# One level of Strassen's algorithm in the last stage of a hybrid encoder block, with activations passed through DRAM

## The chip, the cores and the metric

The kernel runs on one core of a Trainium2 chip. The time is the device time of one launch in microseconds (us). PE is TensorE (matmuls), DVE is VectorE, ACT is ScalarE, POOL is GpSimd, SP is SyncE, which here only issues DMAs. SBUF is the on-chip memory of 128 partitions, PSUM the accumulators that matmuls write, DRAM the memory outside the core.

## The reference, cut to what matters

Sequence 2048, width 1024, feed-forward width 4096, all float32.

```python
mix = jnp.concatenate([att.reshape(bsz, s, ATTN_WIDTH), ssm], axis=-1)   # each 512 wide
h = h + mix @ w_out[l]                                # 1024 x 1024
hn2 = rmsnorm(h, norm2_g[l])
h = h + jnp.square(jax.nn.relu(hn2 @ w_mlp1[l])) @ w_mlp2[l]   # 1024 x 4096, 4096 x 1024
return rmsnorm(h, final_g)
```

`att` is the attention output after an RMS norm over each head's 128 values; `ssm` is `z * sigmoid(z @ w_glu + b_glu)`, the gate. Both are made in earlier stages.

## The kernel before

Four stages follow each other, each a block with its own queues for the five engines: the projection, attention, the state space model with its gate (`phase_ssm`), and the last stage (`phase_mlp`), which computes the lines above. Only the last part of `phase_ssm` and the whole of `phase_mlp` are changed.

Values are kept transposed: features on the 128 partitions, tokens along the columns. Every float32 product of the last stage is made of three matmuls in the faster format fp32r: a value is split into a high part (ACT copies it with rounding) and a low part (DVE subtracts the high part from the value), and high x high, high x low and low x high are added in PSUM.

`phase_mlp` goes through four blocks of 512 tokens (`tb`). In each, `out` makes eight 128-row tiles of `mix @ w_out` and adds `x`; then come two halves of the feed-forward layer: 16 pieces `up` (1024 to 128 features, then relu squared) and two times eight pieces `down`, which collect in four PSUM banks. All activations of a block stay in SBUF. The weights are read once per block of tokens, in pieces of 128x1024 (512 KB) through four buffers `w_raw`; ACT and DVE split each piece (`split_high`, `split_low`) while TensorE uses the one before it. POOL squares and adds `h` for the norm, 128x512 at a time, and issues the loads of `mix` and `x` and the stores of `y`. The norm's factor is applied after `up` and `down`, since relu squared scales with its square, and so stands in nobody's way.

The attention outputs reach the stage with tokens on the partitions. DVE scales them (`mix_scale`), TensorE turns them in four 128x128 transposes a head (`turn_mix`), ACT copies them back with the gain (`mix_back`); for the blocks after the first this lies beside the `up` and `down` pieces.

The gate, the end of `phase_ssm`, has 16 rounds (4 blocks of tokens x 4 tiles of features): TensorE makes `z @ w_glu` into `y_ps`, ACT the sigmoid into `gate`, DVE the product with `z` into `out`, SP stores `out` to `ssm_s`. `y_ps`, `gate` and `out` have two buffers each.

Engines take their instructions in the order in which they are written, and wait for semaphores in that order too.

Of the kernel before, what the change touches and what calls it, by code (L numbers as in the profile page):

```python
# [7 lines left out]

# [8 lines left out]
F32 = mybir.dt.float32  # L17
# [7 lines left out]
P = 128  # L25
# [1122 lines left out]
def phase_ssm(nc, head, mag, s_d, cp_s, w_glu, b_glu, z_s, ssm_s):  # L1148
# [13 lines left out]
    NPAIR = NGR * 2  # L1162
    with ExitStack() as ctx:
# [21 lines left out]
        out = m.sb("out", [P, 2, TB])  # L1185
        w_ps = m.ps("w_ps", [P, 2, 2, NJ])
# [27 lines left out]
        out_stored = [m.sem("out_stored0"), m.sem("out_stored1")]  # L1214
        block = ctx.enter_context(nc.Block())
# [32 lines left out]
        def _(sp):  # L1248
# [21 lines left out]

            sp.dma_start(d_in[:], s_d).then_inc(d_loaded, 16)
# [4 lines left out]
            for n in range(NGR):  # L1276
# [11 lines left out]
                if n == 3:  # L1288
                    sp.dma_start(wg[:], w_glu).then_inc(glu_loaded, 16)
                    sp.dma_start(bg[:], b_glu).then_inc(glu_loaded, 16)  # L1290
                if n + XR < NGR:
# [8 lines left out]
            for n in range(4 * NTB):  # L1300
                tb, c = n // 4, n % 4
                sp.wait_ge(out_ready, n + 1)
                sp.dma_start(ssm_s[c, :, tb * TB:(tb + 1) * TB], out[:, n % 2]).then_inc(out_stored[n % 2], 16)
            for i in range(2):
                sp.wait_ge(out_stored[i], 16 * 2 * NTB)

# [35 lines left out]
        def _(act):  # L1342
# [29 lines left out]

            for t in range(4):
                turned_b(0, t)
# [13 lines left out]
            for n in range(4 * NTB):  # L1388
# [4 lines left out]
                    .then_inc(gate_ready, 1)  # L1393

        @block.vector
        def _(dve):
# [25 lines left out]

            for step in range(NPAIR + 3):
# [9 lines left out]
            for n in range(4 * NTB):  # L1433
# [4 lines left out]
                if n >= 2:  # L1438
# [4 lines left out]
                    .then_inc(out_ready, 1)  # L1443

        @block.tensor
        def _(pe):
# [69 lines left out]
            for n in range(NGR - 3, NGR):  # L1516
                outputs(n)
            pe.wait_ge(glu_loaded, 32)
            for n in range(4 * NTB):
# [9 lines left out]
                last.then_inc(glu_done, 1)  # L1529


def phase_mlp(nc, x_t, att_s, att_square, att_floor, ssm_s, w_stream, gains, y_t):
# [13 lines left out]
    PIECE = 1024  # L1546
    RAW = 4
    TURNS = 18
    OUT_TURNS, UP_TURNS, DOWN_TURNS = 2, 4, 2
    HALF_TURNS = UP_TURNS + 2 * DOWN_TURNS  # L1550
    OUTS, DOWNS = OUT_TURNS * RAW, DOWN_TURNS * RAW
    MIX_ORDER = list(range(H, KD)) + list(range(H))
    Y_TILES = {5: (0, 1, 2), 6: (3, 4, 5), 7: (6, 7)}
    NC = TB // P
    LAM_INIT = 0.8 - 0.6 * math.exp(0.0)
    with ExitStack() as ctx:
        m = Memory(nc, ctx, "ml")
        w_raw = m.sb("w_raw", [P, RAW, PIECE])
        w_hi = m.sb("w_hi", [P, 2, PIECE], F32R)
        w_lo = m.sb("w_lo", [P, 2, PIECE], F32R)  # L1560
        act_hi = m.sb("act_hi", [P, 16, TB], F32R)
        act_lo = m.sb("act_lo", [P, 16, TB], F32R)
        hg_hi = m.sb("hg_hi", [P, KD, TB], F32R)
        hg_lo = m.sb("hg_lo", [P, KD, TB], F32R)
        h = m.sb("h", [P, KD, TB])
        x_in = m.sb("x_in", [P, KD // 2, TB])
        h_out = m.sb("h_out", [P, KD, TB])
        mix = m.sb("mix", [P, KD, TB])
        relu = m.sb("relu", [P, 2, TB])
        relu_sq = m.sb("relu_sq", [P, 2, TB])  # L1570
        product_in = relu_sq
        square = m.sb("square", [P, TB])
        sums = m.sb("sums", [P, TB])
        square2 = m.sb("square2", [P, TB])
        sums2 = m.sb("sums2", [P, 2, TB])
        inv_var = m.sb("inv_var", [P, TB])
        total = m.sb("total", [P, H, S // P])
        rinv_att = m.sb("rinv_att", [P, H, NC])
        inv_c = m.sb("inv_c", [P, NC])
        rms_c = m.sb("rms_c", [P, NC])  # L1580
        gain = m.sb("gain", [P, 2 * KD + 1])
        gain_att = m.sb("gain_att", [P, 1])
        ones = m.sb("ones", [P, 1])
        ident = m.sb("ident", [P, P])
        eps_c = m.sb("eps_c", [P, 1])
        work = m.ps("work", [P, 2, TB])
        down = m.ps("down", [P, 4, TB])
        spread = m.ps("spread", [P, 2, TB])
# [48 lines left out]
        def static(x):  # L1637
            return isinstance(x, int)
# [621 lines left out]
```

## Time and profile before

| | us |
|---|---|
| time, median of 3 runs | 2972.96 |
| lowest and highest of them | 2971.13, 4062.39 |
| span of the profiled execution (first to last instruction) | 2969.5 |
| last stage, from SP's first DMA issue to the end of the span | 1315.2 to 2969.5 |
| its matmuls, first start to last start | 1331.5 to 2940.3 |
| busy in the span: PE / DVE / ACT / POOL | 2781.0 / 1696.7 / 1196.7 / 358.4 |

The profiled execution's own time isn't listed beside the three; its span is 1.6 us under the lowest of them and 3.5 us under the median. Busy time of PE is not time at full speed: matmuls overlap in the pipeline, so what one costs is read from the distance between starts.

### The profile page before, as it was taken

What the parts mean: (1) busy time and instruction counts of PE and PEld (TensorE: products, weight loads), DVE (VectorE), ACT (ScalarE), POOL (GpSimd) and SP (SyncE); (2) the same over time, 40 slices, a digit from 0 to 9 for tenths busy, and PEclk for the clock granted to TensorE, in tenths of its full rate; (3) what the DMA queues carried; (4) which work ended last, traced back from release to release, by engine and by line L of the source; (5) the groups of instructions that cost most, each with busy time, mean ns of one, the idle gap of its engine ahead of it and who ended that gap; (6) DMA issues with size and microseconds to landing.
All of it is one profiled execution on the core that took longest, in us unless ns stands there. A gap on an engine that the chain in (4) does not pass through costs nothing.

```text
span 2969.5 us, 37537 instructions
## 1 busy us (share of the span) xinstructions
PE 2781.0 (94%) x13704; PEld 2319.9 (78%) x13704; DVE 1696.7 (57%) x2363; ACT 1196.7 (40%) x1847; POOL 358.4 (12%) x300
## 2 busy tenths in 40 slices
PE   6978796999999979979999999999999999999996
PEld 5757585999999967737888878888888888788885
DVE  7665517999999947635434365443554343743434
ACT  3365515878787731123323223233233232232331
POOL 5230001101010013303000121000130001300001
PEclk9989898999999989989999999999999999999998
DMA  5335524020220049634232334232252222332322
GB/s 168 139 144 204 183 72 112 22 66 23 65 72 22 17 133 283 165 142 142 92 99 93 98 99 170 92 99 92 93 177 96 95 98 93 101 124 95 99 93 70
DMA packets 160980, 322.41 MB, mean 109 GB/s; under 512 B 30160, under 2 KB 87760, under 8 KB 157136
## 3 DMA queue, kind: packets, MB, share of 16 engines
q1 hardware_dynamic: 143568, 265.58, 29.0%
q10 hardware_dynamic: 10368, 29.89, 2.7%
q0 software_dynamic: 6912, 25.17, 2.3%
q8 instruction: 84, 1.38, 0.2%
q14 instruction: 48, 0.39, 0.0%
HBM read 255.05 MB, written 63.44 MB: 107 GB/s over the span
## 4 chain that ended last, share of the span: by engine, by line
PE 49%; DVE 3%; DMA 1%; issue 1%; POOL 0%; ACT 0%; DVEq 0%; POOLq 0%; ACTq 0%
PE ml_work L2087 9%; PE ml_work L2089 8%; PE ml_work L2088 8%; PE ml_down L2089 8%; PE ml_down L2087 8%; PE ml_down L2088 8%; DMA ml_x_in<-in_x_t 1%; DVE ml_w_lo L1762 1%; PE ml_spread L2050 0%; DVE ml_h L1899 0%; DVE ml_h_out L1888 0%; DMA ml_mix<-att_s 0%; DVE ml_hg_lo L1903 0%; DVE ml_h_out L1974 0%; ACT ml_w_hi L1758 0%
## 5 line engine op out<-in xcount | busy, mean ns | idle before, releaser
L1762 DVE TENSOR_TENSOR ml_w_lo<-ml_w_raw,ml_w_hi 128x1024 fp32r<-128x1024 f32 x288 | 369.1, 1281 | 797.4 <-ACT ml_w_hi L1758 797.3
L1758 ACT ACTIVATE ml_w_hi<-ml_w_raw 128x1024 fp32r<-128x1024 f32 x288 | 305.2, 1060 | 1033.7 <-PE ml_down L2089 542.2
L2087 PE MATMUL ml_work<-ml_hg_hi,ml_w_hi 128*128 128x512 f32 x1024 | 399.5, 390 | 0.8 <-DVE ml_w_lo L1762 0.8
L2087 PE MATMUL ml_down<-ml_act_hi,ml_w_hi 128*128 128x512 f32 x1024 | 399.0, 390 | 0.0
L2089 PE MATMUL ml_work<-ml_hg_hi,ml_w_lo 128*128 128x512 f32 x1024 | 398.5, 389 | 0.0
L2088 PE MATMUL ml_work<-ml_hg_lo,ml_w_hi 128*128 128x512 f32 x1024 | 398.4, 389 | 0.0
L2089 PE MATMUL ml_down<-ml_act_hi,ml_w_lo 128*128 128x512 f32 x1024 | 398.4, 389 | 0.0
L2088 PE MATMUL ml_down<-ml_act_lo,ml_w_hi 128*128 128x512 f32 x1024 | 398.4, 389 | 0.0
L886 ACT ACTIVATE at_e<-at_e,at_neg_top 128x2048 f32<-128x2048 f32 x128 | 256.6, 2005 | 37.0 <-DVE at_neg_top L971 37.0
L1081 PEld LDWEIGHTS at_pv<-at_v,at_a_t 128*128 128x128 f32 x2048 | 257.5, 191 | 16.4
L1081 PE MATMUL at_pv<-at_v,at_a_t 128*128 128x128 f32 x2048 | 258.9, 275 | 0.0
L1054 PE MATMUL at_score<-at_k_hi,at_q_hl 128*128 128x512 f32 x512 | 225.1, 440 | 20.7 <-DVE at_q_hl L948 17.7
L2087 PEld LDWEIGHTS ml_work<-ml_hg_hi,ml_w_hi 128*128 128x128 f32 x1024 | 192.3, 188 | 41.6 <-issue 1.4
L2089 PEld LDWEIGHTS ml_work<-ml_hg_hi,ml_w_lo 128*128 128x128 f32 x1024 | 192.2, 188 | 40.2
L2089 PEld LDWEIGHTS ml_down<-ml_act_hi,ml_w_lo 128*128 128x128 f32 x1024 | 192.3, 188 | 39.9
L2088 PEld LDWEIGHTS ml_down<-ml_act_lo,ml_w_hi 128*128 128x128 f32 x1024 | 192.3, 188 | 39.7
L2088 PEld LDWEIGHTS ml_work<-ml_hg_lo,ml_w_hi 128*128 128x128 f32 x1024 | 192.3, 188 | 39.6
L2087 PEld LDWEIGHTS ml_down<-ml_act_hi,ml_w_hi 128*128 128x128 f32 x1024 | 192.3, 188 | 39.6
L1055 PE MATMUL at_score<-at_k_lo,at_q_hl 128*128 128x512 f32 x512 | 203.5, 397 | 0.0
L691 PE MATMUL pj_acc<-pj_x_hi,pj_w_hi 128*128 128x512 f32 x384 | 156.1, 406 | 49.7 <-DVE pj_x_lo L591 27.3
L964 DVE CUSTOM_DVE_ANT_0 at_e<-at_score,at_bias,at_top 128x1024 f32<-128x1024 f32 x128 | 164.3, 1284 | 41.5 <-PE at_score L1055 29.3
L898 ACT ACTIVATE at_a_t<-at_turned 128x512 f32<-128x512 f32 x256 | 137.7, 588 | 99.1 <-PE at_turned L1067 99.1
(213 smaller groups left out, 4351.7 us busy)
## 6 DMA issues: line engine op xcount, KB each, us to landing
ml_w_raw<-in_w_stream SPq DMA_DIRECT2D x290, 512.0 KB, 3.5
tab_s<-pj_tab ACTq DMA_DIRECT2D x32, 512.0 KB, 2.6
pj_x_raw<-in_x_t SPq DMA_DIRECT2D x14, 1024.0 KB, 8.4
ss_tab<-tab_s SPq DMA_DIRECT2D x17, 512.0 KB, 12.7
pj_w_raw<-in_w_in SPq DMA_DIRECT2D x16, 512.0 KB, 4.2
qk_s<-pj_qku_out SPq DMA_DIRECT2D x32, 256.0 KB, 2.5
at_k_raw<-qk_s SPq DMA_DIRECT2D x16, 512.0 KB, 7.5
at_q_raw<-qk_s SPq DMA_DIRECT2D x128, 64.0 KB, 2.4
```

Of the source, the lines that this page charges most:

```text
L691: pe.matmul(out, w_hi[:, k, cols], x_hi[:, k], start=(k == 0), stop=False)
L886: act.activation(e[:, n % 2, c], e[:, n % 2, c], ACT.Exp, bias=neg_top[:, n % 2, c:c + 1], scale=SCALE, accum_out=esum[:, n % 2, c:c + 1]) ...
L898: act.activation(a_t[:, n % 2, 4 * j:4 * j + 4], turned[:, j % 2].rearrange("p (k q) -> p k q", q=P), ACT.Copy).then_inc(turned_out, 1)
L964: dve.tensor_tensor_reduce(out=e[:, s % 2, c, half * HALF:(half + 1) * HALF], in0=score[:, half], in1=bias[:, at:at + HALF], scale=1.0, sc ...
L1054: pe.matmul(out, q_hl[:, s % 2, c], k_hi[:, h % 2, c, cols], start=True, stop=False)
L1055: last = pe.matmul(out, q_hl[:, s % 2, c], k_lo[:, h % 2, c, cols], start=False, stop=True)
L1081: last = pe.matmul(pv[:, n % 2, 0:P], a_t[:, n % 2, kt], v[:, h % 2, kt], start=(kt == 0), stop=(kt == NQ - 1))
L1758: act.activation(w_hi[:, r % 2], w_raw[:, (r + 2) % RAW], ACT.Copy).then_inc(w_hi_ready, 1)
L1762: dve.tensor_tensor(w_lo[:, r % 2], w_raw[:, (r + 2) % RAW], w_hi[:, r % 2].bitcast(F32), ALU.subtract)\
L2087: pe.matmul(out, lhs_hi, rhs_hi, start=first, stop=False)
L2088: pe.matmul(out, lhs_hi, rhs_lo, start=False, stop=False)
L2089: return pe.matmul(out, lhs_lo, rhs_hi, start=False, stop=last)
```

## The change

**Last stage.** The products become 18 chunks, each a product of 1024 x 1024 weights with 1024 features x 1024 tokens: two for `w_out` (MIX, one for each half of the tokens), and for each half of the tokens four of the first feed-forward matrix (UP) and four of the second (DOWN). Each chunk is made by one level of Strassen's algorithm in Winograd's form. Inputs and weights are cut in 2x2 quarters of 512 x 1024 or 512 x 512 values, each of which lies in SBUF as a tile of 128x2048 (1 MB): `q[Q11]`.. for inputs, `r[R11]`.. for weights. Seven products (steps 0 to 6) of sums and differences of quarters replace eight. A step has four slots, one for each 128-row tile of the result's quarter; a slot is 4 x 3 = 12 matmuls of 128x512. Results gather in two sets of four PSUM banks (`x_ps` for steps 0, 2, 4, 6, `y_ps` for 1, 3, 5).

While TensorE is in step g, ACT and DVE split inputs and weights of step g+1, one half tile (128x1024) in each slot: slot 0 and 1 the input, slot 2 and 3 the weights. A slot of TensorE waits for the splits, and every second one for the weights' half.

**Sums of quarters.** POOL makes all weight sums (8 operations of 128x1024 a chunk) and two of the input differences (4 operations); DVE makes the two others (`first_input`, `second_input`, 4 operations).

**Activations through DRAM.** A chunk's inputs are loaded as four quarters of 1 MB, and the results of MIX, UP and the last DOWN are stored to `h_s`, `act_s` and `h_s` again; the running sum of DOWN stays in `res`. The norm is now applied to `h` itself: squares by ACT, added by POOL, column sums over all partitions in one 128x512 matmul, root by ACT, reciprocal of 128x512 by DVE, then 16 scalings of 128x512 by DVE on tiles read back from `h_s`, stored to `hn_s` (or `y_t`). This lies beside the chunk after: chunks 1, 2 and 10; after chunk 17 it is the end of the kernel.

**Weights** are laid out by quarter, and read twice (once per half of the tokens) in place of four times.

**Attention outputs** are scaled, turned and copied back beside the gate's rounds, and stored to `att_t`.

```diff
@@ phase_ssm, SP @@
+            def load_att(n):
+                wait(sp, att_turned, n - 1)
+                tb, c = n // H, n % H
+                sp.dma_start(att_in[:, n % 2], att_s[c, :, tb * TB:(tb + 1) * TB]).then_inc(att_loaded[n % 2], 16)
...
-            for n in range(4 * NTB):
+            load_att(2)
+            load_att(3)
+            for n in range(NGATE):
                 tb, c = n // 4, n % 4
+                store_att(n)
                 sp.wait_ge(out_ready, n + 1)
                 sp.dma_start(ssm_s[c, :, tb * TB:(tb + 1) * TB], out[:, n % 2]).then_inc(out_stored[n % 2], 16)
+                if n + 4 < NGATE:
+                    load_att(n + 4)
@@ phase_ssm, DVE, in round n, behind the product into out @@
+                if n + 4 < NGATE:
+                    att_scale(n + 4)
@@ phase_ssm, PE, in round n, behind the gate's matmuls @@
+                if n + 2 < NGATE:
+                    turn_att(n + 2)
@@ phase_mlp, SP @@
+            def load_r(k, n):
+                mode, s, c = CHUNKS[k]
+                if k:
+                    prev = (k - 1) * STEPS
+                    if n == R11:
+                        sp.wait_ge(w_lo_ready, 2 * (prev + 2) + 2)
+                        sp.wait_ge(s_ready, 8 * k)
+                    elif n == R21:
+                        sp.wait_ge(w_lo_ready, 2 * (prev + 4) + 2)
+                    elif n == R12:
+                        sp.wait_ge(w_lo_ready, 2 * (prev + 5) + 2)
+                    else:
+                        sp.wait_ge(w_lo_ready, 2 * (prev + 6) + 2)
+                chunk = (0, 1, 5)[mode] + c
+                sp.dma_start(r[n][:], w_stream[chunk, n]).then_inc(r_loaded[n], 16)
@@ phase_mlp, POOL @@
+            def weights(k):
+                for n in range(2):
+                    if n == 0:
+                        pool.wait_ge(r_loaded[R21], 16 * (k + 1))
+                        pool.wait_ge(r_loaded[R22], 16 * (k + 1))
+                        pool.wait_ge(r_loaded[R11], 16 * (k + 1))
                     if k:
+                        pool.wait_ge(w_lo_ready, 2 * ((k - 1) * STEPS + 3) + 1 + n)
+                    pool.tensor_tensor(half(s_first, n), half(r[R21], n), half(r[R22], n), ALU.add).then_inc(s_ready, 1)
+                    pool.wait_ge(s_ready, 8 * k + 3 * n + 1)
+                    pool.tensor_tensor(half(r[R21], n), half(r[R11], n), half(r[R21], n), ALU.subtract).then_inc(s_ready, 1)
+                    pool.wait_ge(w_lo_ready, 2 * k * STEPS + 1 + n)
+                    pool.wait_ge(s_ready, 8 * k + 3 * n + 2)
+                    pool.tensor_tensor(half(r[R11], n), half(s_first, n), half(r[R11], n), ALU.subtract).then_inc(s_ready, 1)
...
+            for k in range(NCH):
+                weights(k)
+                inputs(k)
+                if k and whole(k - 1):
+                    add_squares(k - 1, C21)
+                last_sum(k)
+                last_input(k)
+                if whole(k):
+                    add_squares(k, C11)
+                    add_squares(k, C22)
+                    add_squares(k, C12)
@@ phase_mlp, DVE @@
+            first_input(0, 0)
+            first_input(0, 1)
+            for n in range(4):
+                split_low(0, n)
             dve.wait_ge(gain_loaded, 16)
+            for g in range(NSTEP):
+                k, i = g // STEPS, g % STEPS
+                event = EVENT[k - 1] if k and whole(k - 1) else None
+                for d in range(4):
+                    m_ = 4 * g + d
+                    if m_:
+                        leave((m_ - 1) // 4 // STEPS, (m_ - 1) // 4 % STEPS, (m_ - 1) % 4)
+                    if g + 1 < NSTEP:
+                        split_low(g + 1, d)
+                    if i == 6 and d >= 2 and k + 1 < NCH:
+                        first_input(k + 1, d - 2)
+                    if i == 0 and d < 2:
+                        second_input(k, d)
+                    if kind(k) == UP:
+                        if i == 2 and d in (1, 2):
+                            relu_square(k, C11, d - 1)
+                        if i == 5 and d in (2, 3):
+                            relu_square(k, C22, d - 2)
+                        if i == 6 and d in (1, 3):
+                            relu_square(k, C12, d // 2)
+                    if event is not None:
+                        if (i, d) == (0, 3):
+                            invert(event, 0)
+                        if (i, d) == (3, 0):
+                            invert(event, 1)
+                        if i in (1, 2, 3, 4):
+                            n = 4 * (i - 1) + d
+                            if d == 0:
+                                dve.wait_ge(hb_loaded[(i - 1) % 2], 16 * (2 * event + (i - 1) // 2 + 1))
+                            normalize(event, n, hb[:, (i - 1) % 2, d], KD if kind(k - 1) == DOWN else 0)
@@ phase_mlp, PE @@
+            def slot(k, i, d):
+                g = k * STEPS + i
+                if d == 0:
+                    pe.wait_ge(b_lo_ready, 2 * g + 2)
+                if d % 2 == 0:
+                    pe.wait_ge(w_lo_ready, 2 * g + 1 + d // 2)
+                if i >= 2:
+                    evacuated(pe, k, i - 2, d)
+                elif k:
+                    evacuated(pe, k - 1, 6 if i == 0 else 5, d)
...
+                for kt in range(4):
+                    w = slice((d * 4 + kt) * P, (d * 4 + kt + 1) * P)
+                    b = slice(kt * TB, (kt + 1) * TB)
+                    pe.matmul(out, w_hi[:, w], b_hi[:, b], start=fresh and kt == 0, stop=False, skip_group_check=True)
+                    pe.matmul(out, w_hi[:, w], b_lo[:, b], start=False, stop=False, skip_group_check=True)
+                    last = pe.matmul(out, w_lo[:, w], b_hi[:, b], start=False, stop=kt == 3, skip_group_check=True)
+                last.then_inc(slot_done, 1)
```

`leave` is the evacuation of the slot before from PSUM: DVE adds the bank to `res`; in an UP chunk ACT copies steps 0, 2, 3 and 6. `last_sum` is `R12 - R11` (already summed), `inputs` is `Q22 - Q12`, `last_input` `Q11 - Q21`, each in two halves; `inputs` waits for `first_input`, `last_sum` for the splits of step 1's weights, `last_input` for `second_input` and the splits of step 1's inputs.

## Rows read from the trace of the kernel before

**Rows 1.** The page, part 2: granted clock in 40 slices, in tenths.
```profile
PEclk9989898999999989989999999999999999999998
```
**Rows 2.** Windows: last stage's matmuls, then its tail; busy us (x instructions), clock.
```profile
1331.00:2941.00 1610.00, 1597.20 (x7096) 1320.44 (x7096) 739.00 (x836) 492.98 (x624) 161.03 (x125) 1.00 0.32 106
2941.00:2970.00 29.00, 5.65 (x24) 5.27 (x24) 13.26 (x20) 0.99 (x2) 4.36 (x8) 0.55 0.20 73
```
**Rows 3.** Timeline of PE: start us, us, instruction; twelve matmuls apart.
```profile
1342.10 0.39 PE L2088 MATMUL ml_work<-ml_act_lo,ml_w_hi 128*128 128x512 f32 x1
...
1344.82 0.39 PE L2088 MATMUL ml_work<-ml_act_lo,ml_w_hi 128*128 128x512 f32 x1
```
**Rows 4.** Waits, last stage: us in total, times, longest.
```profile
DVE ml_w_lo L1762 <- ACT ml_w_hi L1758: 797.3, 258, 4.3
...
PE ml_work L2087 <- DVE ml_w_lo L1762: 11.9, 10, 2.2
```
**Rows 5.** Timeline of POOL and DVE around 1345 us.
```profile
1345.56 1.04 POOL L1710 TENSOR_TENSOR ml_square<-ml_h 128x512 f32<-128x512 f32 x1 [4.39 <-DVE ml_h L1899]
...
1345.88 1.80 DVE L1762 TENSOR_TENSOR ml_w_lo<-ml_w_raw,ml_w_hi 128x1024 fp32r<-128x1024 f32 x1 [0.40 <-ACT ml_w_hi L1758]
...
1346.68 2.15 POOL L1713 TENSOR_TENSOR ml_sums<-ml_sums,ml_square 128x512 f32<-128x512 f32 x1
...
1347.61 1.77 DVE L1903 SCALAR_TENSOR_TENSOR ml_hg_lo<-ml_h,ml_gain,ml_hg_hi 128x512 fp32r<-128x512 f32 x1
```
**Rows 6.** Instructions by line: ns min/median/max, first and last start.
```profile
L1762 DVE TENSOR_TENSOR ml_w_lo<-ml_w_raw,ml_w_hi x288: 1207/1226/2239, 1340.4 to 2941.8; 128x1024 fp32r<-128x1024 f32 x144
...
L1758 ACT ACTIVATE ml_w_hi<-ml_w_raw x288: 1041/1061/1069, 1339.4 to 2940.7; 128x1024 fp32r<-128x1024 f32 x144
...
L1899 DVE TENSOR_TENSOR ml_h<-ml_work,ml_x_in x32: 675/691/693, 1339.4 to 2591.1; 128x512 f32<-128x512 f32 x32
...
L1903 DVE SCALAR_TENSOR_TENSOR ml_hg_lo<-ml_h,ml_gain,ml_hg_hi x32: 739/1527/1777, 1342.2 to 2592.5; 128x512 fp32r<-128x512 f32 x32
...
L1734 POOL TENSOR_TENSOR ml_sums<-ml_sums,ml_square x12: 1284/1294/2155, 1691.5 to 2906.4; 128x512 f32<-128x512 f32 x12
```
**Rows 7.** Timelines of SP and PE: the last stage's first issue and first matmul.
```profile
1315.24 0.34 SPq L1659 DMA_DIRECT2D ml_gain<-in_gains  x1
...
1331.53 0.77 PE L2087 MATMUL ml_work<-ml_act_hi,ml_w_hi 128*128 128x512 f32 x1 [0.78 <-DVE ml_act_lo L1876]
```
**Rows 8.** The page, part 6; DMA view of 1313 to 1345 us, 40 slices.
```profile
ml_w_raw<-in_w_stream SPq DMA_DIRECT2D x290, 512.0 KB, 3.5
...
GB/s 105 223 0 0 93 246 353 415 410 425 410 415 374 384 389 389 379 399 394 405 405 282 77 389 307 292 215 31 0 0 0 0 20 0 0 0 0 10 154 394
```
**Rows 9.** Timelines of PE and POOL: the last matmul of the products, the last stores.
```profile
2940.25 0.39 PE L2089 MATMUL ml_down<-ml_act_hi,ml_w_lo 128*128 128x512 f32 x1
...
2956.80 5.15 POOL L1700 DMA_DIRECT2D y_t<-ml_h_out  x8 [49.10 <-DVE ml_h_out L1888]
```
**Rows 10.** Instructions by line, projection stage: reciprocal and column sums of 128x512.
```profile
L596 DVE RECIPROCAL pj_rinv_b<-pj_rms_b x4: 3339/3350/3353, 39.1 to 226.0; 128x512 f32<-128x512 f32 x4
...
L668 PE MATMUL pj_stat_b<-pj_square_sum,pj_ones x8: 592/634/676, 37.0 to 215.2; 128*128 128x512 f32 x8
```
**Rows 11.** The gate's product and its stores; eight transposes in the last stage.
```profile
L1441 DVE TENSOR_TENSOR sm_out<-sm_gate,sm_z_t x16: 1078/1096/1096, 1261.5 to 1311.6; 128x512 f32<-128x512 f32 x16
...
DMA to landing us min/median/max: 2.0/2.1/2.4
...
1959.80 1.04 PE L2068 MATMUL ml_spread<-ml_ident,ml_mix 128*128 128x128 f32 x8
```
**Rows 12.** Windows: a restart of TensorE, and a stretch with a 2.2 us wait.
```profile
1332.00:1336.00 4.00, 4.00 (x11) 3.03 (x11) 3.60 (x6) 1.55 (x3) 0.00 (x0) 0.50 0.55 196
1336.00:1340.00 4.00, 4.00 (x19) 3.32 (x18) 0.65 (x1) 0.65 (x1) 0.00 (x0) 1.00 0.01 4
...
1360.00:1378.00 18.00, 15.79 (x63) 12.55 (x62) 8.68 (x9) 5.13 (x6) 8.49 (x6) 0.91 0.43 144
```

More of the change, by code:

```diff
@@ L9 @@
+import itertools
 import math
@@ L1765, in mix_tiles @@
-        def mix_tiles(half, wide, piece):
-            if half and wide and piece >= 4:
-                return (2 * (piece - 4), 2 * (piece - 4) + 1)
-            return ()
+            for k in range(NCH):
+                weights(k)
[8 more added lines that the diff above has]
+                    add_squares(k, C12)
@@ new lines, in squares @@
+            def squares(k, reg, d):
+                e = EVENT[k]
+                at = SQUARES.index(reg)
+                t = J_T[reg][1]
+                evacuated(act, k, LAST_STEP[reg], d)
+                if at < 2 and d == 0:
+                    if e:
+                        act.wait_ge(stat_done, 2 * e)
+                    dst = sums[:, t]
+                else:
+                    n = 14 * e + (0, 3, 6, 10)[at] + d - (at < 2)
+                    wait(act, added, n - 1)
+                    dst = square[:, n % 2]
+                act.activation(dst, res[reg][:, d], ACT.Square).then_inc(squared, 1)
@@ L2037, in _ @@
+            leave(NCH - 1, STEPS - 1, 3)
+            e = EVENT[NCH - 1]
+            for n in range(16):
+                if n == 0:
+                    invert(e, 0)
+                if n == 8:
+                    invert(e, 1)
+                if n % 4 == 0:
+                    dve.wait_ge(squared, squared_by(e, TILES[n // 4], 3))
+                normalize(e, n, res[TILES[n // 4]][:, n % 4], KD)
         @block.tensor
         def _(pe):
-            def spread_out(bank, column):
-                for c in range(NC):
-                    last = pe.matmul(spread[:, bank, c * P:(c + 1) * P], column(c).to_broadcast([P, P]), ident[:],
-                                     start=(c == 0), stop=(c == NC - 1), skip_group_check=True)
-                return last
@@ new lines, in statistics @@
+            def statistics(e, n):
+                pe.wait_ge(added, 14 * e + (10, 14)[n])
+                k = [k for k in EVENT if EVENT[k] == e][0]
+                if n == 0:
+                    evacuated(pe, k, 5, 3)
+                elif k + 1 < NCH:
+                    evacuated(pe, k + 1, 1, 3)
+                else:
+                    pe.wait_ge(rms_ready, 2 * e + 1)
+                pe.matmul(y_ps[:, 3], ones[:], sums[:, 1 - n], start=True, stop=True).then_inc(stat_done, 1)
+            pe.wait_ge(consts_ready, 2)
@@ L2181, in ssm_layout, with quarters @@
+            statistics(EVENT[NCH - 1], 0)
+            statistics(EVENT[NCH - 1], 1)
+def weight_stream(w_out, w1, w2):
+    def quarters(w):
+        return w.reshape(2, 4, P, 2, 4, P).transpose(3, 0, 2, 4, 1, 5).reshape(4, P, 4 * TB)
+    chunks = [quarters(w_out)]
+    chunks += [quarters(w1[:, c * D:(c + 1) * D]) for c in range(4)]
+    chunks += [quarters(w2[c * D:(c + 1) * D]) for c in range(4)]
+    return np.ascontiguousarray(np.stack(chunks))
 def ssm_layout(inputs):
```

1011 lines of the change are left out of this document (498 added, 513 removed).

## The prediction

> **What bounds the kernel now.** I read the windows by stage first: over the last stage TensorE is busy nearly all the time at the full granted clock [rows 1, 2]. The timeline gives the pitch of its matmuls: the ones that start at 1342.10 and 1344.82 are twelve apart, so one 128x512 product costs 0.2267 us and a group of twelve 2.72 us [rows 3]. The stage has 6912 of them (768 output projection, 3072 up, 3072 down): 1566.7 us, and from the first at 1331.5 to the last at 2940.6 pass 1609 us. The list of waits says the same from the other side: VectorE waits 797 us for the high halves, while TensorE waits for VectorE only 11.9 us [rows 4]. TensorE is the bound, and 42 us of the stage are not matmuls.
>
> **What Strassen removes.** Seven products of quarters in place of eight: 18 chunks x 7 steps x 48 matmuls = 6048, 864 fewer, 864 x 0.2267 = 196 us. A step is 4 slots of 2.72 us = 10.9 us, a chunk 76.2 us, all chunks 1371 us.
>
> **What it adds, engine by engine.** Weights and inputs are now split anew for every step: 28 low halves of 128x1024 a chunk on VectorE, 1.2 us each [rows 6] = 33.6 us, 4 input differences 4.8 us, in an expansion chunk 6 squarings (7 us) and 12 evacuations from PSUM at 0.69 us (8 us), in a contraction chunk 28 evacuations (19 us): 54 to 58 us of 76. ScalarE's 28 high halves take 30 us [rows 6], and its evacuations fit in the rest. The transfers are at most 12 MB a chunk, and 1 MB took 2.6 us at the 405 GB/s of the busiest slices [rows 8]: 31 us of 76, hidden. Each of these alone would fit. GpSimd gets 12 two-input operations of 128x1024 a chunk, and that decides.
>
> **The price of GpSimd's work.** The timeline at 1345 shows it [rows 5]. A GpSimd square runs 1345.56 to 1346.60. A VectorE subtraction of two SBUF tensors starts at 1345.88 and ends at 1347.68, 1.08 us after the square's end. The GpSimd addition that starts at 1346.68 ends at 1348.83, 1.15 us after that subtraction. The next VectorE operation starts at 1347.61, needs 0.74 us by its shortest, and ends at 1349.38, 0.55 us after the addition. So the two take turns, one whole instruction each. Evacuations from PSUM never stretch (675 to 693 ns in 32), subtractions do (1207 to 2239 ns), GpSimd too (1284 to 2155 ns) [rows 6]. A 128x512 addition holds VectorE off for 1.15 us; one of 128x1024 isn't in the trace: at least 1.15 + 0.53 = 1.7 us, if its second half streamed at VectorE's pace (1.08 us for 1024 columns, 0.55 for 512), at most 2 x 1.15 = 2.3. I take 2.2, near the doubling, since GpSimd's own rate is the one that counts. A pair of turns is 2.2 + 1.1 = 3.3 us.
>
> This is what the Trainium skill says in "SBUF — State Buffer", section "SBUF: two separate sides": VectorE with two SBUF inputs and GpSimd arbitrate for one port pair, and the loser blocks for the whole instruction. By that rule, which speaks against this change, the trace agrees. "GPSIMD Engine Reference", section 3.1, gives 4497 ns for an addition of 2048 elements; half of it, an estimate, is 2.25 us, and with it the sum would rise by about 10 us.
>
> **Where it lands.** All weight sums of a chunk wait for its last quarter. That load is issued when the last split of step 5 frees the buffer, about 1 us before step 6 of the chunk before, and lands in 5 to 6 us (half as many bytes: 3.5 us [rows 8]). So GpSimd starts 5 us into step 6 and never rests before its ninth operation, which waits for a split of step 1. Count VectorE's turns from there until the split that step 1 of the next chunk needs: splits of (6,2), (6,3), (0,0), (0,1), (0,2), four input differences, and in an expansion chunk a squaring: 10, or 9 in contraction; GpSimd gets its 8 between them. That split is ready at 5 + 8 x 2.2 + 10 x 1.1 = 33.6 us (32.5). TensorE could start step 1 at 21.8: it idles some 11.8 us. Then four more pairs, 13.2 us, gate step 2: 46.8 (45.7) us where 32.6 was due. From step 2 to 6 nothing is shared, and TensorE keeps its pace. Stalls: 14.2 us per expansion chunk, 13.1 per contraction chunk. Six and eight of them are without a norm beside them: 85 + 105 = 190 us.
>
> Three chunks have a norm beside them: two reciprocals of 3.35 us [rows 10], 16 two-input scalings of some 0.65 us, and GpSimd's 14 additions of squares (10 before its sums, 4 among them), with two waits of TensorE's queue for the sums, everything behind them held. By the same count, turns are 3.4 us for the splits and 1.8 us for scalings against 4 additions: about 24 us of stall each, bounds 14 (all hidden in the idle time already there) and 40; 72 us.
>
> **Ends of the stage.** Before: issue of the first load at 1315.2, first matmul 1331.5 [rows 7]. After: VectorE's first difference needs the fifth 1 MB load: 2 + 5 x 2.6 = 15 us, two differences and three splits 5.9: first matmul at 21 us. The second difference is in front of step 1's splits and waits for the eighth load (23 us), GpSimd's first turns fall there too: 10 us of stall in chunk 0. Tail before: 2940.6 to 2969.5, 29 us [rows 9]. After: evacuation, column sum 0.6, root 0.7 with its table, reciprocal, 8 scalings of 0.67, reciprocal, 8 scalings, store: 5 + 3.4 + 5.4 + 3.4 + 5.4 + 2 = 24 us.
>
> **Gate stage.** The outputs' turning moves here: 64 transposes leave the last stage and come in here (8 in 1.04 us), a wash on TensorE. But VectorE's scaling of tile n+4 now stands behind product n, and its load is issued after that product's store in SP's queue: 1.10 + 0.4 + 2.1 to 2.5 landing + 0.69 = 4.4 us for a round that took 50.1/15 = 3.34 [rows 11]; the next product queues behind it. For 12 rounds that is 13 us at most; the two gate buffers let TensorE run ahead. I take +10, bounds 0 and 20. Scaling, root and reciprocal of the totals hide in the attention-to-SSM gap.
>
> **Sum.** Stage after: 21 + 1371 + 190 + 72 + 10 + 24 = 1688 us, before 2969.5 - 1315.2 = 1654. With the gate: +44 us. The median is 3.5 us over the span, taken as unchanged: 2973 + 44 = 3017 us. Nearly all that Strassen saves is given back as stalls at each chunk's start. Bounds: 0.1 us on each of the 216 GpSimd operations is 22 us (at 1.7 us an operation, the low end, the time would be near 2915, which the range below covers), norms +-30, gate +-10: own range 2975 to 3065.
>
> **Rivals.** (B) The turns cost nothing: GpSimd's operations slip into VectorE's idle quarter, TensorE stays the bound, with 10 us a norm left. For it: 54 to 58 plus 26 us just reach 76 to 84, with evacuations overlapping; against it: the operations come in one bunch where VectorE has most to do. 21 + 1371 + 30 + 24 + 10 - 1654 = -198: 2775 us.
> (D) VectorE is let in more often or the bunch starts later, half the stall goes: about 2890 us. Against: the strict turns of rows 5.
> (C) Slower: the clock. After the idle start the granted clock is 0.5 for 4 us and then full; a wait of 2.2 us is enough for a piece of the next 18 us to be at half [rows 12]. I assume up to 10 matmuls of a restart at half, 2 us more, which lie inside the second wait (2.3 us of room). If each 12 us idle puts a whole step of 48 matmuls at half clock, 48 x 0.2 = 9.6 us, 7 or more a chunk come out: 17 x 7.3 = 124, and 160 if the norms' waits join: 3140 to 3180 us. It decides from about 11 slow matmuls a restart on.
>
> **Chances.** Forecast 0.66, B 0.16, D 0.09, C 0.09. A measurement here tells 2% (59 us) from no change: faster is under 2913, slower over 3032. Of the forecast's 0.66, 0.27 lies over 3032, since what is not modelled mostly adds time. Slower 0.27 + 0.09 = 0.36, faster 0.16 + 0.05 = 0.21, same 0.43. The range 2880 to 3100 takes in D and the low half of C, and leaves out B.
>
> **What would show it.** Right: TensorE idle some 12 us once per chunk, released by a VectorE split; full rate in steps 2 to 6; chunks 89 to 91 us apart; VectorE's two-SBUF subtractions at 3.3 us beside GpSimd, evacuations at 0.69; GpSimd operations of 3.3 us in bunches of 12. Wrong: chunks 76 to 78 us apart (B), matmuls at 0.43 us for whole steps (C), waits on loads at chunk starts, or waits of TensorE on column sums larger than 40 us a norm.

## The result

The changed kernel took 3074.03 us (median, 3069.55 to 3085.66) against 2972.25 us: a ratio of 1.0354, 95% interval 1.034 to 1.0369. One of the four runs of the kernel before took 4062.39 us; the ratio compares the fast runs alone. Slower by 3.5%, where 1.5% was forecast: on the forecast side, inside the wide range of 2880 to 3100 us, but 9 us above the forecast's own range of 2975 to 3065, and 57 us off its value. The profiled execution took 3077.18 us, its span 3075.3.

The page of after, parts 1 and 2:
```profile
PE 2619.9 (85%) x12696; PEld 2164.8 (70%) x12696; DVE 2393.8 (78%) x2589; ACT 1328.6 (43%) x1942; POOL 965.9 (31%) x434
...
PEclk9988898999999989979889999999998999999998
```
The mean share of VectorE is 78% and that of GpSimd 31%: neither number shows a bound. The granted clock now dips in the last stage, where it was full [rows 1]. Windows of after: the last stage's products, chunk 1 (with a norm beside it), one period of the plain contraction chunks; columns as in rows 2:
```profile
1366.05:3053.30 1687.25, 1431.57 (x6061) 1167.09 (x6062) 1418.28 (x1048) 613.02 (x701) 771.83 (x270) 0.92 0.37 138
1454.05:1564.75 110.70, 86.11 (x342) 68.76 (x341) 94.65 (x79) 38.30 (x47) 58.49 (x26) 0.88 0.57 206
2041.00:2131.60 90.60, 79.08 (x338) 64.68 (x337) 76.03 (x61) 27.48 (x29) 37.00 (x13) 0.92 0.25 93
```
Before, TensorE was idle for 13 of 1610 us [rows 2]; now for 256 of 1687. The matmuls are 864 fewer, and the stretch is 78 us longer. Plain contraction chunks (DOWN) are 90.6 us apart (three in a row, twice; the one behind an expansion chunk takes 92.2), plain expansion chunks (UP) 92.0 to 92.3, and 93.7 for chunk 3, which stands behind a chunk with a norm. I took step lengths from the start times of every 48th product; chunk 7 reads 22.3, 13.8, 11.0 and four times 10.9 us. In a contraction chunk nearly the whole loss is in step 0, behind which step 1 is late, and in step 1; in an expansion chunk step 6 is also long, 12.4 us. The longest group of TensorE's waits in the last stage (columns as in rows 4):
```profile
PE ml_y_ps L2233 <- issue: 223.1, 18, 19.0
```
and, from the timeline, the VectorE split before the stall's end, then the two matmuls of chunk 7 that had to wait:
```profile
2058.55 1.21 DVE L2110 TENSOR_TENSOR ml_w_split<-ml_r,ml_w_split 128x1024 fp32r<-128x1024 f32 x1
...
2059.86 0.77 PE L2233 MATMUL ml_y_ps<-ml_b_split,ml_w_split 128*128 128x512 f32 x1 [11.22 <-issue]
2073.68 0.47 PE L2233 MATMUL ml_x_ps<-ml_b_split,ml_w_split 128*128 128x512 f32 x1 [0.30 <-issue]
```
One long stall per chunk at step 1, 18 in all. The releaser "issue" means that the list found no event. But the low half of step 1's weights is ready at 2058.55 + 1.21 = 2059.76, and TensorE starts 0.1 us later. The inputs and weights of step 1 are quarters as they were loaded (`Q21`, `R12`), so TensorE awaits no sum of GpSimd there, only a VectorE that is late. Why it is late is seen on VectorE and GpSimd, whose timelines in after (one fence, VectorE first) are here around the start of chunk 10:
```profile
2304.78 2.18 DVE L2110 TENSOR_TENSOR ml_w_split<-ml_r,ml_w_split 128x1024 fp32r<-128x1024 f32 x1
2306.88 3.41 DVE L2119 TENSOR_TENSOR ml_t_first<-ml_q 128x1024 f32<-128x1024 f32 x1
2310.22 0.68 DVE L2147 TENSOR_TENSOR ml_res<-ml_x_ps,ml_res 128x512 f32<-128x512 f32 x1
2310.82 2.83 DVE L2110 TENSOR_TENSOR ml_w_split<-ml_r,ml_w_split 128x1024 fp32r<-128x1024 f32 x1
2313.57 3.41 DVE L2119 TENSOR_TENSOR ml_t_first<-ml_q 128x1024 f32<-128x1024 f32 x1
...
2305.84 3.37 POOL L1920 TENSOR_TENSOR ml_s_first<-ml_r 128x1024 f32<-128x1024 f32 x1
2309.29 3.27 POOL L1922 TENSOR_TENSOR ml_r<-ml_r 128x1024 f32<-128x1024 f32 x1
2312.71 3.19 POOL L1925 TENSOR_TENSOR ml_r<-ml_s_first,ml_r 128x1024 f32<-128x1024 f32 x1
2315.86 3.38 POOL L1920 TENSOR_TENSOR ml_s_first<-ml_r 128x1024 f32<-128x1024 f32 x1
```
Read them side by side: every GpSimd operation starts with a VectorE operation of two SBUF inputs under way, and the four start 3.45, 3.42 and 3.15 us apart. In each such time VectorE gets through exactly one operation with two inputs in SBUF. The evacuation at 2310.22, whose one input is in PSUM, took 0.68 us with GpSimd at work beside it. By instruction, over the whole run (columns as in rows 6):
```profile
L1920 POOL TENSOR_TENSOR ml_s_first<-ml_r x36: 2395/3372/3466, 1365.2 to 2965.5; 128x1024 f32<-128x1024 f32 x36
...
L1941 POOL TENSOR_TENSOR ml_q<-ml_q x36: 2332/3319/3386, 1384.7 to 2978.8; 128x1024 f32<-128x1024 f32 x36
...
L2147 DVE TENSOR_TENSOR ml_res<-ml_y_ps,ml_res x184: 676/691/693, 1392.4 to 3042.6; 128x512 f32<-128x512 f32 x184
...
L2110 DVE TENSOR_TENSOR ml_w_split<-ml_r,ml_w_split x180: 1208/1218/3440, 1364.7 to 3029.6; 128x1024 fp32r<-128x1024 f32 x180
```

### The profile page after: what moved, and what is told of

Same layout as the page of the kernel before. It is cut to its first block, busy times and chain, and to the rows that moved or that the text cites. A ratio compares the mean times of both kernels' runs of the same rounds, so it can differ in the third digit from the quotient of the medians.

```text
span 3075.3 us, 33940 instructions
## 1 busy us (share of the span) xinstructions
PE 2619.9 (85%) x12696; PEld 2164.8 (70%) x12696; DVE 2393.8 (78%) x2589; ACT 1328.6 (43%) x1942; POOL 965.9 (31%) x434
## 4 chain that ended last, share of the span: by engine, by line
PE 34%; DVE 11%; issue 7%; POOL 3%; ACT 1%; DMA 0%; SPq 0%; DVEq 0%; ACTq 0%; POOLq 0%
PE ml_y_ps L2233 7%; PE ml_y_ps L2234 6%; PE ml_y_ps L2235 6%; PE ml_x_ps L2233 5%; PE ml_x_ps L2234 5%; PE ml_x_ps L2235 5%; DVE ml_b_split L2100 4%; DVE ml_t_first L2119 2%; DVE ml_q L2127 2%; DVE ml_w_split L2110 1%; DVE ml_res L2153 1%; POOL ml_s_first L1920 1%; POOL ml_r L1922 1%; POOL ml_q L1941 1%; DVE ml_rinv L2158 1%
## 5 line engine op out<-in xcount | busy, mean ns | idle before, releaser
L2233 PE MATMUL ml_y_ps<-ml_b_split,ml_w_split 128*128 128x512 f32 x864 | 354.7, 410 | 229.0 <-issue 223.1
L2233 PE MATMUL ml_x_ps<-ml_b_split,ml_w_split 128*128 128x512 f32 x1152 | 455.6, 395 | 52.5 <-DVE ml_w_split L2110 26.4
L2001 ACT ACTIVATE ml_b_split<-ml_q 128x1024 fp32r<-128x1024 f32 x216 | 221.6, 1053 | 639.6 <-PE ml_x_ps L2235 257.0
L2100 DVE TENSOR_TENSOR ml_b_split<-ml_q,ml_b_split 128x1024 fp32r<-128x1024 f32 x216 | 401.6, 1860 | 65.0 <-ACT ml_b_split L2001 63.9
L2234 PE MATMUL ml_x_ps<-ml_b_split,ml_w_split 128*128 128x512 f32 x1152 | 451.2, 392 | 0.0
L2235 PE MATMUL ml_x_ps<-ml_b_split,ml_w_split 128*128 128x512 f32 x1152 | 450.9, 391 | 0.0
L2233 PEld LDWEIGHTS ml_y_ps<-ml_b_split,ml_w_split 128*128 128x128 f32 x864 | 171.9, 199 | 273.3 <-issue 236.9
L2234 PE MATMUL ml_y_ps<-ml_b_split,ml_w_split 128*128 128x512 f32 x864 | 350.6, 406 | 0.0
L2235 PE MATMUL ml_y_ps<-ml_b_split,ml_w_split 128*128 128x512 f32 x864 | 348.9, 404 | 0.0
L2110 DVE TENSOR_TENSOR ml_w_split<-ml_r,ml_w_split 128x1024 fp32r<-128x1024 f32 x180 | 318.8, 1774 | 37.9 <-ACT ml_w_split L2019 37.9
L1920 POOL TENSOR_TENSOR ml_s_first<-ml_r 128x1024 f32<-128x1024 f32 x36 | 111.3, 3090 | 708.0 <-DMA ml_r<-in_w_stream 708.0
L2233 PEld LDWEIGHTS ml_x_ps<-ml_b_split,ml_w_split 128*128 128x128 f32 x1152 | 218.0, 189 | 107.7 <-issue 62.0
L1082 PEld LDWEIGHTS at_pv<-at_v,at_a_t 128*128 128x128 f32 x2048 | 257.5, 191 | 16.4
L2235 PEld LDWEIGHTS ml_x_ps<-ml_b_split,ml_w_split 128*128 128x128 f32 x1152 | 218.1, 189 | 45.9
L2234 PEld LDWEIGHTS ml_x_ps<-ml_b_split,ml_w_split 128*128 128x128 f32 x1152 | 218.0, 189 | 46.0 <-issue 1.4
L2019 ACT ACTIVATE ml_w_split<-ml_r 128x1024 fp32r<-128x1024 f32 x216 | 218.7, 1046 | 0.2 <-POOL ml_r L1925 0.2
L2235 PEld LDWEIGHTS ml_y_ps<-ml_b_split,ml_w_split 128*128 128x128 f32 x864 | 171.0, 198 | 37.5
```

The costliest lines, as they stand in the source:

```text
L1082: last = pe.matmul(pv[:, n % 2, 0:P], a_t[:, n % 2, kt], v[:, h % 2, kt], start=(kt == 0), stop=(kt == NQ - 1))
L2001: act.activation(half(b_split[:, g % 2, 0], h), half(src, h), ACT.Copy).then_inc(b_hi_ready, 1)
L2019: act.activation(half(w_split[:, g % 2, 0], h), half(src, h), ACT.Copy, scale=-1.0 if i == 6 else 1.0)\
L2100: dve.tensor_tensor(half(b_split[:, g % 2, 1], h), half(src, h), half(b_split[:, g % 2, 0], h).bitcast(F32), ALU.subtract).then_inc(b_lo_r ...
L2110: dve.tensor_tensor(lo, half(src, h), hi.bitcast(F32), ALU.subtract).then_inc(w_lo_ready, 1)
L2233: pe.matmul(out, w_hi[:, w], b_hi[:, b], start=fresh and kt == 0, stop=False, skip_group_check=True)
```

## The experiments

The first four ran on one chip (the kernel before there: 2969.91 us), the last four on another (2971.95). What they have to tell apart: whether the stall is GpSimd's turns, whether the gate stage holds what the forecast missed, and what is behind the norm.

**Gate queue.** In the gate stage SP issues the next load and the store after next before it waits for a product.
```diff
+            store_att(0)
+            store_att(1)
             for n in range(NGATE):
                 tb, c = n // 4, n % 4
-                store_att(n)
-                sp.wait_ge(out_ready, n + 1)
-                sp.dma_start(ssm_s[...], out[:, n % 2]).then_inc(out_stored[n % 2], 16)
                 if n + 4 < NGATE:
                     load_att(n + 4)
+                if n + 2 < NGATE:
+                    store_att(n + 2)
+                sp.wait_ge(out_ready, n + 1)
+                sp.dma_start(ssm_s[...], out[:, n % 2]).then_inc(out_stored[n % 2], 16)
```


> Of the changed kernel, only SP's order in the gate stage is edited: the load of attention tile n+4 and the store of tile n+2 are issued before SP waits for gate product n, not behind it. Theory (the 86 us from the first gate matmul to the last stage's first DMA issue are rounds of 5.2 us, set by load and store latencies that stand behind the product in SP's queue): rounds fall to TensorE's own 3.9 us (3.43 for the gate's matmuls, 0.45 for four transposes), the stretch to about 65 us, the time by 18 to 22 us, to about 3053 us. Rival (VectorE's scaling or the transposes themselves set the round): no more than 5 us. The last stage keeps its chunks of 90.6 and 92.2 us.

3057.6 us, ratio 1.0298 (1.028 to 1.0315): 16.4 us under the changed kernel, where 18 to 22 were expected. In after, the waits from the first gate matmul to the last stage, then SP's round, which repeats:
```profile
DVE sm_att_in L1475 <- DMA sm_att_in<-att_s: 52.8, 13, 6.8
ACT sm_att_out L1412 <- DMA att_t<-sm_att_out: 51.0, 13, 4.9
```
```profile
1293.58 0.32 SPq L1336 DMA_DIRECT2D ssm_s<-sm_out  x1
1293.94 0.43 SPq L1291 DMA_DIRECT2D sm_att_in<-att_s  x1
1294.42 0.44 SPq L1296 DMA_DIRECT2D att_t<-sm_att_out  x1
1298.93 0.32 SPq L1336 DMA_DIRECT2D ssm_s<-sm_out  x1
```
In the kernel with the queue edit, the same waits (ScalarE's wait for the store is gone from the list) and the same round:
```profile
DVE sm_att_in L1478 <- DMA sm_att_in<-att_s: 22.1, 13, 6.1
```
```profile
1290.73 0.32 SPq L1341 DMA_DIRECT2D ssm_s<-sm_out  x1
1293.19 0.32 SPq L1291 DMA_DIRECT2D sm_att_in<-att_s  x1
1294.05 0.32 SPq L1296 DMA_DIRECT2D att_t<-sm_att_out  x1
1294.60 0.32 SPq L1341 DMA_DIRECT2D ssm_s<-sm_out  x1
```
The round fell from 5.35 to 3.87 us, and from the first gate matmul to the end of the stage it is 67.5 us instead of 86.35; before it was 61.3. The chunks stayed as they were (90.6 and 92.2). So 18.9 of the 25 us by which the gate's stretch had grown were the order in SP's queue. The load landed 3.5 us after its issue in the median, and 2.7 with the edit. The edit moves the load and the store together; their shares weren't taken apart.

**Narrow sums.** GpSimd's twelve sums and differences of a chunk on 64 of 1024 columns: the order and all waits stay, nearly all of the work is left out.
```diff
-                    pool.tensor_tensor(half(s_first, n), half(r[R21], n), half(r[R22], n), ALU.add).then_inc(s_ready, 1)
+                    pool.tensor_tensor(part(s_first, n), part(r[R21], n), part(r[R22], n), ALU.add).then_inc(s_ready, 1)
```


> GpSimd's twelve sums and differences of each chunk are made on 64 columns of each half in place of 1024, with all waits and the order kept; the sums are so left out almost wholly, and the matmuls work on partly unsummed quarters. Theory (turns at the SBUF port): the operations hold VectorE for some 0.2 us in place of 2.25, so the 12 us wait of TensorE at step 1 and the 2 to 3 us at step 2 go; plain chunks fall from 90.6 to 92.2 us to 76 to 78, chunks with a norm from 103 to 111 to 85 to 95, chunk 0 to about 80: 2790 to 2820 us. Rival (the chunk's start waits for loads that come late, or VectorE's own order is too long for the slots): plain chunks stay above 86 us, time above 2980.

2780.44 us (one execution). Window of the products, then VectorE's input splits among the groups by line in it (columns: busy us, mean ns, idle before and its releaser):
```profile
1366.00:2770.00 1404.00, 1384.58 (x6059) 1140.41 (x6057) 1056.15 (x1058) 612.44 (x705) 242.03 (x268) 0.99 0.45 166
```
```profile
L2105 DVE TENSOR_TENSOR ml_b_split<-ml_q,ml_b_split 128x1024 fp32r<-128x1024 f32 x214 | 263.2, 1230 | 85.1 <-ACT ml_b_split L2006 83.2 <-DMA ml_gain<-in_gains 0.8
```
Every plain chunk is 76.2 us and every step 10.9: that is the pace of the sum's 1371 us, so in the plain chunks the loads, the splits and the waits between engines cost nothing here. With the same 214 splits, VectorE needs 263.2 us in place of 399.2 (mean 1866 ns in after). With nothing changed but the size of GpSimd's operations, 294 us go. The norms cost 11, 6 and 3 us there. This run alone doesn't say whether TensorE waited for the sums themselves or for a VectorE that is held off; the next two tell them apart.

**Late half.** GpSimd's three late pairs (input differences and last weight sum) start only behind the weight split of step 2, which cuts the bunch in two. 
```diff
                 weights(k)
-                inputs(k)
                 if k and whole(k - 1):
                     add_squares(k - 1, C21)
+                pool.wait_ge(w_lo_ready, 2 * (k * STEPS + 2) + 2)
+                inputs(k)
                 last_sum(k)
```


> Of the changed kernel, GpSimd's last six operations of a chunk (two input differences in halves, the last weight sum) wait until step 2's weights are split; nothing is left out. Theory: six turns in place of eight stand before the split that step 1 waits for, none of GpSimd's before the one of step 2; step 0 to 1 falls from 22.3 to about 17 us and step 1 to 2 from 13.8 to 11 or 13 (cold clock), some 6 to 8 us a chunk, and steps 2 to 4, where VectorE has 0.9 us of idle time in a slot, take the six at a price of 0 to 3 us. 17 chunks x 4 to 7 us = 70 to 120 us less, 2955 to 3005 us. Rival (TensorE waits because the sums themselves are ready late, not because VectorE is held): the first six are no earlier than before and the last six later, so the time stays or rises, 3070 to 3120 us.

3047.1 us, ratio 1.0265 (1.0248 to 1.0282): 27 us less, and 70 to 120 were expected. The rival, that TensorE waits for late sums, is out: six of the twelve now come later, and step 1 starts 3.7 us earlier. Plain contraction chunks fell from 90.6 to 85.6 (steps 18.6, 12.6, then 10.9), expansion chunks hardly moved (91 to 92: steps 19.0, 13.8, 13.0, 12.3): there VectorE also has six squarings, and the late half of the bunch takes its turns from steps 2 and 3. Chunks 9 and 17 even rose to 92.4. The waits in chunk 9 (the longest is the last number) say why:
```profile
POOL ml_sums L1960 <- ACT ml_square L2053: 24.1, 2, 20.9
...
ACT ml_square L2053 <- POOL ml_sums L1960: 14.3, 3, 13.6
...
DVE ml_w_split L2111 <- ACT ml_w_split L2020: 9.3, 1, 9.3
```
One of ScalarE's squares waits 13.6 us for GpSimd's additions, now queued behind the late bunch; behind that square on its engine stands the high half of a weight, behind this VectorE's low half. Moving turns moves the stall; the size of my expectation took the moved half as free.

One step isolates the clock: step 1 of these contraction chunks has no GpSimd operation beside it until its last 0.7 us and no wait of TensorE behind its first matmul, and takes 12.6 to 12.8 us in place of 10.9. Windows of this kernel's chunk 7, in the stall, then after its first matmul at 2046.62:
```profile
2040.00:2046.00 6.00, 0.00 (x0) 0.00 (x0) 6.00 (x6) 2.18 (x3) 0.83 (x1) 0.81 0.00 0
2046.00:2050.00 4.00, 3.38 (x8) 2.77 (x9) 3.98 (x5) 1.82 (x2) 0.00 (x0) 0.50 0.00 0
2050.00:2054.00 4.00, 4.00 (x17) 3.22 (x17) 1.82 (x2) 0.00 (x0) 0.00 (x0) 0.93 0.00 0
```
After an idle time of 7.5 us the granted clock is at its lower level, 1.2 GHz, for some 4 us: 1.7 to 1.9 us lost.

**Sums on VectorE.** All twelve move from GpSimd to VectorE, two to a slot in the first two steps and one to a slot later; GpSimd keeps the norm's squares.
```diff
-                weights(k)
-                inputs(k)
...
+                    for what in {(0, 2): ['A0', 'A1'], (0, 3): ['B0', 'B1'], (1, 0): ['C0'], (1, 1): ['C1'], ...}.get((i, d), ()):
+                        quarter_sum(k, what)
...
+                    dve.tensor_tensor(half(s_first, n), half(r[R21], n), half(r[R22], n), ALU.add).then_inc(s_ready, 1)
```


> All twelve sums and differences of a chunk are moved from GpSimd to VectorE, spread over slots (0,2) to (3,3); nothing is left out. VectorE's own work rises to 66 to 70 us of a 76 us chunk. Theory (turns): an operation costs VectorE 1.15 us there in place of the 2.25 us for which GpSimd holds it off, and no bunch forms: plain chunks 77 to 80 us, chunks with a norm 88 to 98 (16 scalings and 8 sums beside each other), 3074 - 14 x 13 - 3 x 14 - 8 = about 2840 us, 2815 to 2880. Rival (VectorE's load sets the chunk, whoever makes the sums): more work on it makes plain chunks 90 us or more, 3070 or slower.

2842.96 us, ratio 0.9575 (0.9559 to 0.959): 231 us under the changed kernel, and faster than the kernel before. Its window of a plain chunk, and a line of VectorE (columns as in rows 6):
```profile
2025.80:2102.40 76.60, 76.42 (x337) 62.99 (x336) 67.96 (x73) 27.57 (x28) 0.00 (x0) 1.00 0.29 110
```
```profile
L2106 DVE TENSOR_TENSOR ml_w_split<-ml_r,ml_w_split x180: 1203/1216/2312, 1358.6 to 2793.9; 128x1024 fp32r<-128x1024 f32 x180
```
VectorE has twelve instructions more than in after's chunk (73 for 61) and is busy for 68.0 us instead of 76.0. Without the twelve, 68.0 - 12 x 1.22 = 53.4 us are left; so with GpSimd at work, VectorE spent 76.0 - 53.4 = 22.6 us more on the same instructions. An operation costs VectorE 1.2 us if it does it itself, and 1.9 us if GpSimd does it. The kernel with narrow sums bears this out; its window of the same chunk has VectorE's 61 instructions of after in 56.0 us, 20 less, with GpSimd's twelve cut short:
```profile
1992.12:2068.28 76.16, 76.16 (x337) 63.07 (x336) 56.03 (x61) 27.34 (x28) 6.86 (x13) 1.00 0.30 111
```
The whole time is as expected, but the chunks with a norm took 102.6, 99.3 and 98.1 us, where 88 to 98 were expected.

**Combined.** The gate queue's edit and the one before this, with nothing else; their diffs stand above.

> The two edits that helped alone, together: the twelve sums of a chunk on VectorE, and in the gate stage the next load and the store after it issued ahead of the wait for the product. They touch different stages, so if both causes are what I take them for their gains add: 2842.96 less the 16.4 to 18.9 of the queue edit, 2824 to 2827 us. Rival: the gate's stretch was only so long because of something that the start of the last stage hides again (VectorE now has more to do from its first chunk on), so that part of it is lost: 2835 to 2843.

2827.9 us, ratio 0.9516 (0.95 to 0.9532), 1 us above the expected range: the gains add up, 15 of the 16 us of the gate edit are kept. It beats both kernels.

**Split work.** The six early weight sums on VectorE, the six late operations on GpSimd behind the same weight split as in the late half, step 2's (the expectation calls it step 3's).
```diff
+                pool.wait_ge(w_lo_ready, 2 * (k * STEPS + 2) + 2)
                 inputs(k)
...
+                    for what in {(0, 2): ['A0', 'A1'], (0, 3): ['B0', 'B1'], (1, 0): ['C0'], (1, 1): ['C1']}.get((i, d), ()):
+                        quarter_sum(k, what)
```


> The six weight sums that come early in a chunk are on VectorE; the six late ones (last weight sum, both input sums) stay on GpSimd and start behind the weight split of step 3. Theory of turns: each of the six still takes up to 2.25 us away from a VectorE that has about 9 us of room in a chunk of 76.6; 6 x 2.25 = 13.5 against 6 x 1.15 = 6.9 saved, so VectorE is asked for some 6.6 us more than with all on it: it just fits or goes over by a few us. Plain chunks of 77 to 83 us, whole kernel 2850 to 2930, not better than all on VectorE. Rival: GpSimd works in the gaps that VectorE has anyway, so moving half of the work off VectorE gives a faster kernel than all on it, 2835 or less.

2921.35 us, ratio 0.9832 (0.9816 to 0.9848): 78 us slower than with all of them on VectorE. Plain expansion chunks 82.4 to 83.8, contraction chunks 78.6, and chunks 0, 9 and 17 take 86.6 to 87.2, with the chain through ScalarE's square again; these three hold some 29 of the 78 us. The rival, that GpSimd's work fits into VectorE's gaps, is out: giving half of the work away costs time.

**Narrow squares, narrow reciprocals.** The combined kernel with GpSimd's 14 additions of squares per norm on 32 of 512 columns, and with the reciprocals on 64 of 512.
```diff
-                    pool.tensor_tensor(sums[:, t], sums[:, t], square[:, done % 2], ALU.add).then_inc(added, 1)
+                    pool.tensor_tensor(sums[:, t, 0:32], sums[:, t, 0:32], square[:, done % 2, 0:32], ALU.add).then_inc(added, 1)
...
-                dve.reciprocal(rinv[:, 1 - n], rinv[:, 1 - n]).then_inc(rinv_ready, 1)
+                dve.reciprocal(rinv[:, 1 - n, 0:64], rinv[:, 1 - n, 0:64]).then_inc(rinv_ready, 1)
```


> The combined kernel with the 14 additions of squares that GpSimd does per norm cut to 32 of 512 columns (nearly all of the norm's sums is left out). Theory: these additions are GpSimd operations with two inputs in SBUF and take turns with VectorE too; their 25.3 us of a norm chunk come out of VectorE's time there. Chunks 1, 2 and 10, 102.6, 99.3 and 98.1 us with the full additions, fall to 82 to 90 us, the whole by 30 to 50. Rival: what is long in these chunks is VectorE's own work for the norm (two reciprocals of 3.35 us, scaling), then they stay above 95.

> The combined kernel with the two reciprocals of each norm on 64 of 512 columns (the other columns are left as square roots). Each falls from 3.35 us to about 0.4: theory of a full VectorE: chunks 1, 2 and 10 fall by up to 5.9 us each, the whole by 10 to 18. Rival: the reciprocals lie where VectorE had room, the chunks fall by under 2 us each.

Chunks 1, 2 and 10 take 102.1, 99.4 and 98.5 us in the combined kernel, 95.5, 97.8 and 95.1 with narrow additions (11.6 us in all), 95.3, 95.0 and 91.2 with narrow reciprocals (18.5 in all; up to 5.9 each expected). One execution each: 2817.45 and 2805.22 us, 10 and 23 us under the combined kernel (30 to 50 and 10 to 18 expected). Neither expectation was met. With narrow additions all three chunks stay above 95 us, as the rival has it: most of what is long there isn't GpSimd's additions. In chunks 1 and 10 the reciprocals cost 6.8 and 7.3 us, more than their own length. The windows of chunk 1, combined, then narrow additions, then narrow reciprocals, each in its own kernel:
```profile
1425.50:1527.60 102.10, 85.86 (x342) 68.51 (x340) 92.21 (x90) 38.77 (x47) 24.38 (x13) 0.90 0.61 225
```
```profile
1425.80:1521.30 95.50, 82.80 (x341) 66.47 (x340) 83.11 (x90) 38.78 (x47) 8.99 (x14) 0.95 0.64 236
```
```profile
1422.70:1518.00 95.30, 83.78 (x342) 66.37 (x341) 85.45 (x90) 39.01 (x47) 23.99 (x13) 0.95 0.63 237
```
VectorE's busy time falls by 9.1 and by 6.8 us, and the chunk by 6.6 and 6.8. In all three VectorE is at rest for 10 to 12 us of a chunk and TensorE for more, so neither is the bound alone: the stalls are where one waits for the other in the norm's chain. Of the 70 us by which these three chunks are longer than plain ones, the two edits, each alone, name 30; the other 40 I did not take apart.

## What the prediction had right, and the steps that failed

**The mechanism held.** Strict turns, one whole instruction each, with the bunch at the chunk's start: in contraction chunks step 1 starts 33.2 us after step 6 of the chunk before (forecast 32.5), step 2 at 47.0 (45.7). Narrow sums and sums on VectorE show it as the cause, from two sides. Rival B lost by its cause too: with narrow sums the plain chunks take the 76.2 us that B gives them. That its 2775 us agree so well with the 2780 measured there is in part luck, since the gate's growth, 16 us above B's 10, is set off by 11 us less in other terms. Rival D lost: in plain chunks the bunch started 4.1 to 4.6 us into step 6 (one at 6.7), where 5 was counted.

Rival C lost, but not by its count. At a restart 7 to 12 matmuls of a plain chunk lie about 0.43 us apart, and four chunks reach the 11 from which it was to decide. In contraction chunks these 1.6 to 2.6 us lie inside the wait for step 2, as assumed: 0.2 to 1.2 us of that wait are left. In expansion chunks nothing of it is left; there step 1 takes 12.8 to 13.1 us by the clock alone.

**The 61.8 us that were missing** (the span grew by 3075.3 - 2969.5 = 105.8, forecast 44). The forecast of +44 failed as a sum: three terms were too small, and no other term set them off.

- Gate stage, the term that left its bounds: forecast +10, bounds 0 to 20; the last stage's first issue came at 1344.65 instead of 1315.24 [rows 7], +29.4, of which 25 in the gate stretch. The ring was named rightly, load behind the product's store, but its landing was taken as 2.1 to 2.5 us, from the stores before [rows 11]; here three transfers are issued back to back and the load landed after 3.5. And that only 12 rounds would grow, since TensorE runs ahead, was wrong: 15 intervals between products took 5.10 us each (1264.4 to 1341.0), 3.34 before. ScalarE waited 51 us for the store of the turned tile, a wait that I hadn't priced at all. 19.4 us missing.
- Plain chunks, the largest gap in us: a stall of 190 us was forecast, 216 came. The 25.7 us are more than the 22 that the range allowed for the price of GpSimd's operations, and that price wasn't the fault: in chunk 7 GpSimd's eighth operation ends 30.2 us after the start of step 6, where the sum has 30.3. A contraction chunk is 90.6 us long (forecast 89.3) by what the count left out: VectorE's evacuations. One of 0.6 us stands in front of the split for step 1, and the four pairs in front of step 2, with four evacuations between VectorE's splits, take 13.8 us, not 13.2. An expansion chunk is 92.2 (90.4): "From step 2 to 6 nothing is shared, and TensorE keeps its pace" was wrong there. The bunch begins in step 6, where VectorE also has two squarings, and the first matmul of the chunk behind waits 1.3 to 1.6 us. The contraction chunk behind an expansion chunk is as long, 92.2, and chunk 3 takes 93.7.
- Chunks with a norm: 316.8 us, forecast 300.6. 16.2 us, within the bounds (14 to 40 us of stall each; they are 34.5, 26.6 and 27.2).
- Chunk 0 took 88.0 us (86.2), the start 21.4 (21), the tail 22.0 (24; its terms as written add up to 24.6). Together 0.2 us. (The busiest slices of rows 8 moved 425 GB/s, not 405; nothing hangs on it.)
- The median lies 1.3 us under the profiled span, forecast 3.5 over, which takes 4.8 us back.

**The rule on the port, held against the runs.** The Trainium skill, "SBUF — State Buffer", section "SBUF: two separate sides", says that the one of the two engines that comes second is blocked for the whole instruction; these runs agree: in a contraction chunk GpSimd's first eight operations start 3.26 us apart in the mean, each with one of VectorE's between. For VectorE it names, beside its faster modes, operations with two inputs in SBUF; the evacuations, with one of theirs in PSUM, took 676 to 693 ns in 184, with GpSimd beside them or not.

## What to carry to other kernels

Before work is given to GpSimd "because it is idle", count it as VectorE's time: each 128x1024 operation with two SBUF inputs took 1.9 us of VectorE's time, and VectorE does it itself in 1.2. A busy share may be partly waiting for turns: with twelve instructions more a chunk and no sharing, VectorE was busy for 8 us less. When a ring of load, use and store is threaded into a stage, issue what is ready ahead of the wait for the product, and price the landing from transfers issued back to back.

## What I had not expected of the hardware

GpSimd's operations on 64 of 1024 columns took 0.31 to 0.33 us with no two-input operation of VectorE beside them, where a sixteenth of 2.33 us (the shortest with 1024) is 0.15, and up to 1.38 us beside one (377 to 1079 ns in the mean by line); a narrow operation is not a free one. And a stall of 7.5 us costs TensorE 1.7 to 1.9 us more when it comes back, since the first 4 us are granted half the clock.
